# A two-layer hybrid model on one core: order of VectorE's work in the state-space stage, weight rests, and a bank held longer

## The reference

```python
# first block: layer 0 is a state-space mixer, layer 1 differential attention
for layer in range(2):
    x = x + mixer(x)             # mamba2_mixer or diff_attention
    x = x + conv_ffn(x, ...)
# second block
h = rms_norm_2(x, mix_norm_g)
merged = gate0*(conv @ w0) + gate1*(fox @ w1) + gate2*(swa @ w2)
x = x + merged @ w_mix_out
x = x + cross_attention(rms_norm_2(x, g), rms_norm_2(mem, g2), w_xq, w_xkv, w_xo)
x = x + swiglu(rms_norm_2(x, g3), w_gate, w_up, w_down)
return rms_norm_2(x, final_norm_g)
```

```python
z, xbc, dt = split(rms_norm(x, ln_g) @ in_w)
xbc = silu(causal_dwconv(xbc, conv_w, conv_b))
decay_in = exp(segsum(a))                                   # from differences of cumulated sums
y_diag = einsum('bclgn,bcsgn,bgrcls,bcsgrp->bclgrp', C, B, decay_in, x*dt)
y_off  = einsum('bclgn,bcgrpn,bgrcl->bclgrp', C, states_in, exp(a_cs))
y = (y_diag + y_off + x*d_skip) * silu(z)
out = rms_norm(y in 4 groups, norm_g) @ out_w
```

## Time and profile before

| | us |
|---|---|
| median of 3 runs | 2474.78 (2470.24 to 2475.61) |
| time of the profiled execution | 2476.58 |
| its span | 2474.7 |
| TensorE busy | 2418.3 (98%) |
| VectorE busy | 1406.6 (57%) |
| ScalarE busy | 969.7 (39%) |
| GpSimd busy | 409.2 (17%) |

### The profile page before, as it was taken

How to read it: one execution, slowest core, us unless ns; L and a number is a source line. 1 busy time by engine, 2 the same in 40 slices (tenths; PEclk the granted TensorE clock), 3 DMA queues, 4 the chain that set the end, 5 groups by cost and what they waited for, 6 DMA issues and landing times.

```text
span 2474.7 us, 30257 instructions
## 1 busy us (share of the span) xinstructions
PE 2418.3 (98%) x11894; PEld 1961.7 (79%) x11894; DVE 1406.6 (57%) x2286; ACT 969.7 (39%) x1589; POOL 409.2 (17%) x323
## 2 busy tenths in 40 slices
PE   7999999999999999999999999999999999999997
PEld 5777777888888887788888877787787877888886
DVE  6977886663665455576456547534554545443343
ACT  5443434442444444454334334324433434322223
POOL 0341433220111222122002100001201101110012
PEclk9999999999999999999999999999999999999998
DMA  4542222223323221132232332231233322323322
GB/s 151 106 99 70 75 69 85 94 90 101 99 83 121 65 69 60 41 117 94 90 106 89 91 120 81 77 101 53 64 100 131 128 94 86 99 89 102 102 80 82
DMA packets 74301, 226.22 MB, mean 91 GB/s; under 512 B 7856, under 2 KB 12080, under 8 KB 74032
## 3 DMA queue, kind: packets, MB, share of 16 engines
q1 hardware_dynamic: 67968, 212.01, 26.7%
q10 hardware_dynamic: 6192, 12.29, 2.4%
HBM read 215.87 MB, written 8.39 MB: 91 GB/s over the span
## 4 chain that ended last, share of the span: by engine, by line
PE 57%; DMA 1%; DVE 1%; ACT 0%; issue 0%; POOL 0%; DVEq 0%; POOLq 0%
PE bank L1102 56%; PE bank L1106 1%; DMA t<-spill 0%; DVE t L1892 0%; ACT t L1455 0%; POOL t L2460 0%; DMA t<-in_mem 0%; ACT t L1458 0%; DVE t L1895 0%; DVEq L2678 0%; DVE t L2388 0%; DVE t L1899 0%; DVE t L2394 0%; POOLq L724 0%; DVEq L724 0%
## 5 line engine op out<-in xcount | busy, mean ns | idle before, releaser
L1102 PE MATMUL bank<-t 128*128 128x512 f32 (+4 forms) x11404 | 2388.5, 375 | 34.9 <-DVE t L1892 28.9
L1102 PEld LDWEIGHTS bank<-t 128*128 128x128 f32 (+1 forms) x11404 | 1909.9, 186 | 474.2 <-issue 93.7
L1455 ACT ACTIVATE t<-t 128x1024 fp32r<-128x1024 f32 (+4 forms) x646 | 548.5, 859 | 691.9 <-PE bank L1102 279.4
L1892 DVE TENSOR_TENSOR t<-t 128x1024 fp32r<-128x1024 f32 (+7 forms) x690 | 634.1, 929 | 256.9 <-ACT t L1455 251.1
L2460 POOL TENSOR_TENSOR t<-t 128x512 f32<-128x512 f32 (+5 forms) x243 | 368.4, 1523 | 1668.3 <-ACT t L1458 567.0
L1892 DVE TENSOR_TENSOR t<-bank,t 128x512 f32<-128x512 f32 (+4 forms) x410 | 275.4, 675 | 485.8 <-PE bank L1102 462.7
L1458 ACT ACTIVATE t<-t 128x512 f32<-128x512 f32 (+5 forms) x545 | 330.4, 616 | 542.1 <-DVE t L1892 344.4
L1895 DVE SCALAR_TENSOR_TENSOR t<-t 128x512 f32<-128x512 f32 (+5 forms) x430 | 322.9, 757 | 97.7 <-ACT t L1458 52.8
L1455 ACT ACTIVATE t<-bank 128x512 f32<-128x512 f32 (+4 forms) x151 | 72.3, 495 | 132.1 <-PE bank L1106 90.7
L2463 POOL TENSOR_SCALAR t<-t 128x128 f32<-128x128 f32 (+3 forms) x64 | 40.2, 633 | 389.0 <-ACT t L1455 254.2
L1106 PE MATMUL bank<-t 128*128 128x128 f32 x490 | 78.5, 276 | 11.3 <-POOL t L2460 3.7
(11 more groups left out here) (25 smaller groups left out, 57.4 us busy)
## 6 DMA issues: line engine op xcount, KB each, us to landing
t<-in_w SPq DMA_DIRECT2D x306, 512.0 KB, 3.4
t<-in_w SPq DMA_DIRECT2D x48, 384.0 KB, 3.1
t<-in_w SPq DMA_DIRECT2D x56, 320.0 KB, 3.0
t<-in_w SPq DMA_DIRECT2D x24, 256.0 KB, 3.0
tab<-t ACTq DMA_DIRECT2D x1, 2560.0 KB
t<-in_x SPq DMA_DIRECT2D x8, 256.0 KB, 6.4
t<-tab SPq DMA_DIRECT2D x8, 256.0 KB, 3.9
spill<-t ACTq DMA_DIRECT2D x1, 2048.0 KB, 8.4
```

The source lines that it names most:

```text
L1102: return eng.matmul(out, lhs, rhs, start=start, stop=stop, skip_group_check=loose)
L1455: return eng.activation(out, in_, ACT.Copy, scale=scale)
L1892: return eng.tensor_tensor(out, a, b, o)
```

## The change

There are three edits in it.

1. In the VectorE program of the state-space stage the multiply of the bank `bo` (pair of age 4) stands in front of the eight subtractions of the pair of age 1, in place of behind them.
2. VectorE writes the rest of a weight unit three ticks after the split tick, not two. This holds for all 444 units in all stages. ScalarE's copy and SyncE's load keep their ticks.
3. The planner holds the bank of the sums of squares of a group for four ticks in place of two. All keys of the other norms keep two.

```diff
     def rms(self, key, g=1):
         n = 4 if g == 1 else 5
-        if not self.place([(("rs", key), 0, 2), (("rb", key), n, 2)]):
+        if not self.place([(("rs", key), 0, 4 if key[0] == "g" else 2), (("rb", key), n, 2)]):
...
+        for g, p in at("pair", T - 4):
+            e_ = buf.ep[(4 * g + p) % 2]
+            w.wait_ge(*full(("bo", g, p)))
+            w.wait_ge(*empty(("s0", g, p)))
+            w.wait_ge(*empty(("s1", g, p)))
+            tt(e_[:, P:S], K.of(("bo", g, p))[:, P:S], e_[:, P:S], MUL).then_inc(*leave(("bo", g, p)))
         for g, p in at("pair", T - 1):
             n = 4 * g + p
             for k in range(2):
...
-        for g, p in at("pair", T - 4):
-            e_ = buf.ep[(4 * g + p) % 2]
-            w.wait_ge(*full(("bo", g, p)))
-            w.wait_ge(*empty(("s0", g, p)))
-            w.wait_ge(*empty(("s1", g, p)))
-            tt(e_[:, P:S], K.of(("bo", g, p))[:, P:S], e_[:, P:S], MUL).then_inc(*leave(("bo", g, p)))
...
         end(T)
-        for u in plan.split_at.get(T - 2, ()):
+        for u in plan.split_at.get(T - 3, ()):
             if u < len(plan.units):
```

## The result

The changed kernel takes 2482.14 us as the median of 7 runs (2479.84 to 2487.41), the kernel before in the same comparison 2475.61 (2470.24 to 2477.74, 7 runs). The ratio is 1.0033, with a 95% interval of 1.0023 to 1.0044: slower by 0.33%, some 8 us by the ratio and 6.5 by the two medians. The forecast was 2483.0, slower, with a range of 2472.5 to 2488.5.

What follows compares the result with a forecast made beforehand. TensorE, busy 98% of the span, was taken as the bound. State-space stage −8.65, start +3.2, attention output +10.3 and two outputs +3.3 sum to +8.15 us on the 2474.78 median: 2483.0, range 2472.5 to 2488.5.

Steps and rivals of the forecast that it cites:

- Start, +3.2: First matmul: unit 0's weight rest, one tick later, stands behind two input rests and two sums; +3.2 us, bounds 2.7 and 3.3.
- State-space stage, −8.65: All three edits together in the state-space stage: waits of TensorE and falls of its clock go; −8.65 us, bounds −5 and −14.
- group 1 (−3.0): Wait at 151.56 and its clock fall go, −4.33 us, with 1.3 given back at a later product; −3.0, bounds −2 and −4.3.
- the bank (−4.45): Wait of 3.19 us at 206.41 and its clock fall go, 0.45 lost at GpSimd's power; −4.45, bounds −3.5 and −4.9.
- the shorter one (−0.35): A shorter wait of the sums-of-squares bank's sort, at group 2's first product, goes; −0.35 us.
- Groups 0, 2 and 3: Other head groups of the state-space stage, same pattern, less to win: −0.2, −0.3 and −0.35 us (group 3 at 352.56).
- new waits of over 1 us at TensorE between 340 and 370 for VectorE: State-space stage: one of the observations that the prediction said would show it wrong.
- Attention output, +10.3: Second half, 1046 to 1066: each rest meets GpSimd's operation, seven periods +1.5 us each, less 0.2 slack; bounds +3.8 and +12.3.
- Two outputs, +1.65 each: Last units of state-space and cross-attention outputs: rests meet GpSimd, the last subtraction comes late; +3.3 us together, bounds 0 and +4.
- four places: Start, attention output's second half, last units of state-space and cross-attention outputs: no slack covers the later rests outside the state-space stage.
- VectorE would win the race: Rival: in the three output places VectorE's rest starts before GpSimd; attention output +3.8, two outputs 0; 2473.1 us, chance 0.24.
- Nothing of the multiply's gain: Rival: later subtractions hold up exponentials and products; state-space −5 or less, race lost; 2486.6 or 2488.5 us, chance 0.04.

## Why the prediction was right

**Start, +3.2.** Right: 3.23. The two subtractions and three operations behind them (the third of them unit 0's rest) are seen on VectorE from 12.38 on, ending at 16.25, the forecast's number.

```profile
12.38 1.41 DVE L1895 SCALAR_TENSOR_TENSOR t<-t 128x512 fp32r<-128x512 f32 x2
13.71 2.54 DVE L1892 TENSOR_TENSOR t<-t 128x512 f32<-128x512 f32 x3
```

**State-space stage, −8.65.** Right as a sum, −8.8, and partly by luck. Near are −2.9 for group 1 (−3.0), −4.6 for the bank (−4.45) and −0.4 for the shorter one (−0.35). Groups 0, 2 and 3 came out at +0.4, −1.4 and +0.2 for −0.2, −0.3 and −0.35: each is off, and the errors cancel. The giving back at the later product, 1.3 in the forecast, is the wait of 1.28 at 166.05. What the experiments corrected is whose gain it is. The forecast put 2.1 of the wait at 151.56 to the multiply and 0.6 to the rests. Alone, the multiply gives nothing over the stage and the rests give −7.5; in group 1 the rests alone give −3.8, and the multiply takes 0.9 of it back. The rest of the weights was the longer part of the queue in front of the multiply, and it was also in front of other operations, whereas moving the multiply let TensorE run ahead of GpSimd and put the subtractions later.

**A sign of being wrong that did come.** The prediction named "new waits of over 1 us at TensorE between 340 and 370 for VectorE". There is one, 2.97 long, at 360.8 of the old axis, with a fall of the clock behind it. It doesn't overturn the sum: the term for group 3 itself counted on 2.26 and 1.7 being given back at the next product, and they were, to +0.2. Term and sign didn't fit each other, and the sign was ill chosen.

**Attention output, +10.3.** The mechanism was right and is shown: a rest that meets GpSimd lasts 1.65, the adds are 3.70 apart, and 2.61 with the race the other way. The count was wrong. The forecast had seven periods longer by 1.5, 10.5 in all. In the trace five are longer, from the add at 1049.61 to the one at 1068.60: 18.99 in place of 11.12, +7.9, one of them 4.15 long because TensorE's clock was low. TensorE's waits there grew by 8.6, from 1.6 to 10.1, and two falls of the clock, which the forecast had only in its bound, gave the other 3.4. So 12.1 against 10.3 is a term too high by about 2 and one left out; that they lie so near is luck. The price of the race won, +3.8, was near (+3.5 measured), though its own terms, seven periods of 0.4 and 0.5 at the first wait, give 3.3.

**Two outputs, +1.65 each.** Right: 1.7 and 1.7, a wait of 1.43 for the last subtraction in both. In the state-space output it ends at 429.29, where the forecast, moved to the axis of after, has 429.31.

**Not foreseen.** The last units ahead of the attention norm (787 to 796) have the same order and cost +0.8, the wait of 0.56 at 790.66. The text held that outside four places the slack covers the move; this was a fifth. Nor was the shorter wait at 1894.71, −1.6. Falls of the clock that come and go between executions (1458, 1895, 1940, 982) made about −3 in this pair of traces, and the slow matmuls at the start −1.1. Together with the attention output (+1.8) they make most of the difference between +8.15 and +6.6.

**Rivals.** That VectorE would win the race did not happen in any of the three places. "Nothing of the multiply's gain" had a chance of 0.04 as a part of a slower case; as a statement on the multiply by itself it was right, and the loss in group 0 fits the mechanism that it names.

## What to carry to other kernels

An age that is moved for all units is a different edit in every stage: the same one-tick delay gave about −4 to −8 where VectorE's queue was late and +12 where a producer on another engine stood at the same instant. Look at who starts within 0.1 us of an operation in its new place, and whether the two block each other. A wait that is removed by reordering one engine is worth only what the slowest engine of the same chain can follow; measure each part of a bundled change alone, since here one of three did nearly all the harm and, in one stage, much of the good, and one did nothing on the whole.

## What the runs showed of the hardware

A VectorE operation with two inputs in SBUF that comes 0.03 us behind a GpSimd operation of 1.27 ends 0.41 behind that one's end: 1.65 for 0.55. A difference of 0.5 us in a third engine turns it to 0.55. The clock fell after some waits of about 1.7 and not after others of the same length: behind the same wait of 1.66 or 1.67 (in front of 980.21 after, of 984.43 before) it fell in five of thirteen traces. And from 13 to 18 us TensorE did 12 matmuls in one kernel and 15 in another with the same program there.
